# Experts 0 and 1 get their token columns by products with one-hot matrices; projection tiles and the second expert stream are requested in and right behind the scan

## The reference, cut to what matters

```
grp_prob = softmax(hf @ w_grp + b_grp);  grp = argmax(...)       # 4 groups
exp_logits = (hf @ w_exp + b_exp) of the chosen group            # 8 experts in it
top_logit, top_idx = lax.top_k(exp_logits, 2)
weights = p_grp * softmax(top_logit)
out[slot] = (silu(x[slot] @ w_gate[e]) * (x[slot] @ w_up[e])) @ w_down[e]
y = sum over the two chosen experts of weight * out
```

## Time and profile before

| | |
|---|---|
| median of 3 executions | 3174.89 us (3172.99 to 3177.99) |
| the profiled execution, its own time | 3174.74 us |
| its span, first to last instruction | 3173.0 us |
| TensorE busy | 2725.0 us (86%), weight loads 1970.6 us |
| VectorE, ScalarE, GpSimd busy | 1072.1, 527.9, 324.9 us |
| DMA | 638.61 MB, mean 201 GB/s |
| mean granted TensorE clock | 0.943 |

### The profile page before, as it was taken

How to read it: one execution, slowest core, us unless ns; L and a number is a source line. 1 busy time by engine, 2 the same in 40 slices (tenths; PEclk the granted TensorE clock), 3 DMA queues, 4 the chain that set the end, 5 groups by cost and what they waited for, 6 DMA issues and landing times. The chain is left out here.

```text
span 3173.0 us, 59030 instructions
## 1 busy us (share of the span) xinstructions
PE 2725.0 (86%) x25835; PEld 1970.6 (62%) x25835; DVE 1072.1 (34%) x2214; ACT 527.9 (17%) x1149; POOL 324.9 (10%) x358
## 2 busy tenths in 40 slices
PE   8999999989999997878786599798899976977775
PEld 7886766678868775444443244588888964544443
DVE  4563336435733213100001321565565422100002
ACT  1001132300011002000000100344444411000001
POOL 1000000000000001111110200232222201111110
PEclk9999998999999997989999799799999987999998
DMA  8684432057864237999998220000000049999994
GB/s 281 228 255 137 130 113 94 27 184 249 264 202 147 80 110 296 391 405 402 401 403 329 77 78 24 13 4 3 3 4 3 4 139 360 404 407 408 406 404 179
DMA packets 297238, 638.61 MB, mean 201 GB/s; under 512 B 29252, under 2 KB 198423, under 8 KB 262436
## 3 DMA queue, kind: packets, MB, share of 16 engines
q1 hardware_dynamic: 254896, 558.44, 48.2%
q10 hardware_dynamic: 30500, 61.96, 5.4%
q0 software_dynamic: 11600, 14.59, 1.5%
HBM read 634.79 MB, written 21.08 MB: 207 GB/s over the span
## 5 line engine op out<-in xcount | busy, mean ns | idle before, releaser
L2502 PE MATMUL bank<-expert_weights,ex_xt 128*64 128x256 f32 x2560 | 310.0, 390 | 74.3 <-DMA expert_weights<-in_moe_w_up_dram 52.6
L546 PE MATMUL bank<-u,weights 128*128 128x272 f32 (+1 forms) x1408 | 318.4, 390 | 11.3 <-DVEq L569 11.3
L2502 PEld LDWEIGHTS bank<-expert_weights,ex_xt 128*64 128x64 f32 x2560 | 203.3, 141 | 183.6 <-issue 113.9
L546 PEld LDWEIGHTS bank<-u,weights 128*128 128x128 f32 x1408 | 270.6, 192 | 58.9 <-DVEq L569 11.9
L1353 DVE SCALAR_TENSOR_TENSOR ada_acc<-ada_w,cond,ada_acc 128x512 f32 (+1 forms) x336 | 227.6, 746 | 1.6 <-PEq L518 1.6
L2420 DVE TENSOR_TENSOR ex_hidden<-ex_silu,bank 128x256 f32<-128x256 f32 x64 | 27.0, 421 | 569.7 <-ACT ex_silu L2551 569.7
L623 PE MATMUL bank<-rw_mixed,weights 128*128 128x512 f32 (+2 forms) x448 | 189.3, 584 | 31.9 <-DVEq L636 28.2
L2502 PE MATMUL bank<-weights,ex_xt 128*64 128x256 f32 x1280 | 165.9, 400 | 33.4 <-DMA weights<-in_moe_w_up_dram 24.4
L2523 PE MATMUL bank<-expert_weights,ex_hidden_turned 128*64 128x512 f32 x640 | 154.7, 626 | 20.7 <-DVE ex_hidden_turned L2423 20.7
L623 PEld LDWEIGHTS bank<-rw_mixed,weights 128*128 128x128 f32 (+1 forms) x448 | 84.2, 189 | 137.4 <-issue 135.5
L2551 ACT ACTIVATE ex_silu<-bank 128x256 f32<-128x256 f32 x64 | 24.6, 384 | 869.0 <-PE bank L2502 853.5
(11 more groups left out here) (602 smaller groups left out, 4292.2 us busy)
## 6 DMA issues: line engine op xcount, KB each, us to landing
expert_weights<-in_moe_w_gate_dram SPq DMA_DIRECT2D x80, 1024.0 KB, 24.4
expert_weights<-in_moe_w_up_dram SPq DMA_DIRECT2D x80, 1024.0 KB, 24.5
expert_weights<-in_moe_w_down_dram SPq DMA_DIRECT2D x80, 1024.0 KB, 24.6
ada_w<-in_ada_w_dram ACTq DMA_DIRECT2D x24, 2048.0 KB, 9.2
weights<-in_moe_w_down_dram SPq DMA_DIRECT2D x44, 1024.0 KB, 24.1
weights<-in_moe_w_gate_dram SPq DMA_DIRECT2D x40, 1024.0 KB, 23.9
weights<-in_moe_w_up_dram SPq DMA_DIRECT2D x40, 1024.0 KB, 24.0
weights<-in_ga_w_in_dram SPq DMA_DIRECT2D x32, 1024.0 KB, 5.7
```

The source lines that it names most:

```text
L546: last = nc.tensor.matmul(k.bank[b + side * NB][:, 0:N], w[:, f, c * P:(c + 1) * P], rhs[:, f, 0:N], start=(f == 5), stop=(f == 4))
L2502: last = nc.tensor.matmul(half_cols(k.bank[2 + side], t), xt[:, s, f * SLOTS:(f + 1) * SLOTS], w[:, q * 512 + t * 256:q * 512 + t * 256 + ...
```

## The change

In both mixtures:

- Experts 0 and 1 no longer get their rows by an inversion, a gather from DRAM and transposes. The token rows stay on chip (`hrow`: all but the last two blocks of 128 tokens in `h`, the last two in `xg`, which now has 128 partitions). For e = 0, 1 VectorE makes `chosen_by[:, e]`, a one-hot of the place times "assigned to e", and TensorE multiplies each row block (128x128 weights, per f and t) with it (64 moving columns), summed over the row blocks in banks 1 and 2. ScalarE copies the two results to `xt`, which now lives in `Route`. With T = 512 there are four row blocks, with T = 256 two.
- ScalarE copies and stores all row blocks without waiting for a buffer, and computes the exponentials afterwards. All stores count one semaphore, `ring.stored`.
- The inversion moves into expert 0 of the expert stage, behind its gate and up products; `tokens` and `pairs_of` are made there, then gathers 2 and 3 run, ahead of the scatters of slot lists. TensorE waits for them ahead of expert 1's down products. Tile 19 is requested at the head of the expert stage in layer 0, and in layer 1 at the head of the route stage.
- The slot lists are filled from a 64-wide memset tile by a DMA of shorter rows; the memset of `xg` goes.

In layer 1 only: the scan's scratch is named by the slots of `wo`, and a SyncE program in the scan's own block requests the four `wo` tiles once `rt_made` and `powered` have counted all heads; the empty block behind goes. The memory of the scan is released first, so `Route` and `place` come ahead of the projection, and the projection's SyncE program starts with the router's weights and 14 expert tiles.

```diff
@@ class ExpertRing, begin
-                for j in range(RING - tiles) if t == 0 else ():
-                    self.start(sp, a, l, 0, j)
                 self.start(sp, a, l, 0, RING - tiles + t)
@@ route_stage
-        hrow = k.h[:, :, :].rearrange("p c t -> p (c t)")[:, 0:2 * D].rearrange("p (s d) -> p s d", s=2)
+        h = k.h[:, :, :].rearrange("p c t -> p (c t)")
+        hrow = [h[:, t * D:(t + 1) * D] for t in range(TT - 2)] + [route.xg[:, t, :] for t in range(2)]
@@ route_stage, sync
-            route.load(sp)
-            for e in range(1, 3):
+            if l == 0:
+                route.load(sp)
+            for e in range(1, 3) if l == 0 else ():
...
-            for b in range(2):
-                sp.wait_ge(rstored[b], 16 * (TT // 2))
-            ring.start(sp, a, l, 3, 0)
+            if l == 1:
+                ring.start(sp, a, l, 3, 0)
@@ route_stage, tensor
-            pe.wait_ge(listed, 2)
-            for half in range(2):
-                for t in range(TT):
-                    for c in range(2):
-                        last = nc.tensor.matmul(k.bank[7][half * SLOTS:(half + 1) * SLOTS, 0:2 * NE], here[:, t, c, :],
...
+            pe.wait_ge(rcopied, 2 * TT)
+            for e in range(2):
+                pe.wait_ge(picked, e + 1)
+                for f in range(DC):
+                    for t in range(TT):
+                        last = nc.tensor.matmul(k.bank[1 + e][:, f * SLOTS:(f + 1) * SLOTS],
+                                                hrow[t][:, f * P:(f + 1) * P], chosen_by[:, e, t, :],
+                                                start=(t == 0), stop=(t == TT - 1))
+                last.then_inc(gathered, 1)
@@ route_stage, scalar
-                    if t >= 2:
-                        act.wait_ge(rstored[t % 2], 16 * (t // 2))
...
+            exponentials(act)
...
-            for b in range(2):
-                act.wait_ge(rstored[b], 16 * (TT // 2))
+            for e in range(2):
+                act.wait_ge(gathered, e + 1)
+                nc.scalar.activation(route.xt[:, e, :], k.bank[1 + e][:, :], ACT.Copy)
@@ route_stage, vector
             dve.wait_ge(placed, 1)
+            for e in range(2):
+                link(nc.vector.tensor_tensor(chosen_by[:, e, :, :], route.for_tokens(place[:, :], SLOTS),
+                                             pos[:, :, e:e + 1].broadcast_to([P, TT, SLOTS]), ALU.is_equal))
+                nc.vector.tensor_tensor(chosen_by[:, e, :, :], chosen_by[:, e, :, :],
+                                        A[:, :, e:e + 1].broadcast_to([P, TT, SLOTS]), ALU.mult).then_inc(picked, 1)
@@ experts_stage, sync
+            if l == 0:
+                sp.wait_ge(ring.stored, ring.rows)
+                ring.start(sp, k.a, l, 3, 0)
@@ experts_stage, vector
+                if e == 0:
+                    dve.wait_ge(inverted, 1)
+                    nc.vector.tensor_scalar(route.tokens[:, :], ...)
+                    nc.vector.tensor_scalar(route.pairs_of[:, :], ...).then_inc(named, 1)
@@ experts_stage, gpsimd
+            pool.wait_ge(named, 1)
+            pool.wait_ge(ring.stored, ring.rows)
+            for e in range(2, 4):
+                gather(k, route, pool, e)
             pool.wait_ge(destined, route.placed)
@@ experts_stage, tensor
-            turn(0)
             for e in range(NE):
...
-                if e + 1 < NE:
+                if e == 0:
+                    invert()
+                elif e + 1 < NE:
                     turn(e + 1)
...
+                if e == 1:
+                    pe.wait_ge(named, 1)
@@ rwkv
         scan_heads(k, q, r, kx, v, lw, la, gate)
-        with nc.Block() as block:
-            block.sync(k.stream.resume)
+        ctx.close()
+        route, ring = Route(k, 1, SEQ, held), k.ring
+        behind = ring.begin(k, a, 1, seg["wo"], 4)
+        ring.place(k, more)
+
+        def early(sp):
+            route.load(sp)
+            for n in [*range(RING - 4), *range(RING, ring.SLOTS - 1)]:
+                ring.start(sp, a, 1, *divmod(n, ring.PIECES))
@@ scan_heads
+            @block.sync
+            def _(sp):
+                sp.wait_ge(scan.rt_made, 2 * DC)
+                sp.wait_ge(scan.powered, 2 * DC)
+                k.stream.resume(sp)
```

More of the change, by code:

```diff
@@ L2177, in _ @@
                     .then_inc(consts, 1)
-            pool.memset(route.xg[:, :, :], 0.0).then_inc(consts, 1)
-            pool.wait_ge(consts, 17)
+            pool.wait_ge(consts, 16)
             pool.wait_ge(zeroed, 16)
-            pool.wait_ge(named, 1)
-            for b in range(2):
-                pool.wait_ge(rstored[b], 16 * (TT // 2))
-            for e in range(2):
-                gather(k, route, pool, e)
         @block.tensor
@@ L2254, in _ @@
             for t in range(TT):
-                if t == TT - 2 and TT > 2:
-                    exponentials(act)
                 for half in range(2):
@@ L2265, in _ @@
                 act.wait_ge(rcopied, 2 * t + 2)
[L2266 to L2268 removed]
+                act.dma_start(route.rows[t * P:(t + 1) * P, :], hrow[t]).then_inc(ring.stored, 16)
+            exponentials(act)
             act.wait_ge(diffed, 1)
             nc.scalar.activation(route.stat(5), route.stat(4), ACT.Exp).then_inc(exped, 1)
[L2271 to L2272 removed]
+            for e in range(2):
+                act.wait_ge(gathered, e + 1)
+                nc.scalar.activation(route.xt[:, e, :], k.bank[1 + e][:, :], ACT.Copy)
         @block.vector
@@ L2488, in turn, with invert @@
                 last.then_inc(turned, 1)
-            turn(0)
+            def invert():
+                for half in range(2):
+                    for t in range(TT):
+                        for c in range(2):
+                            last = nc.tensor.matmul(
+                                k.bank[7][half * SLOTS:(half + 1) * SLOTS, 0:2 * NE], route.here[:, t, c, :],
+                                route.whom[:, t, c, :], start=(t == 0 and c == 0), stop=(t == TT - 1 and c == 1))
+                last.then_inc(inverted, 1)
             for e in range(NE):
                 s = e % 2
-                pe.wait_ge(copied, e + 1)
+                if e >= 2:
+                    pe.wait_ge(copied, e - 1)
                 for j in range(2):
@@ L2699, in vector, with moe @@
         dve.wait_ge(self.put, count * 16 + 16)
-def moe(k, l, T):
+def moe(k, l, T, route, held, more):
     nc = k.nc
@@ L2705, in moe @@
     parts = [(t0, t1, k.gain2[:, v, :], k.mod[:, v, 3 * DC:4 * DC]) for v, (t0, t1) in enumerate(V)]
-    held, more = ExitStack(), ExitStack()
-    route = Route(k, l, T, held)
     with nc.sbuf_tensor(f"moe_h_{l}", [P, DC, T], F32) as hm:
-        k.ring.place(k, more)
+        if l == 0:
+            k.ring.place(k, more)
         route_stage(k, route, hm, parts)
@@ L2893, in rwkv @@
         linear_stage(k, "wo", seg["wo"], whole_tiles(DC, 256), lambda f: gate[:, f, :], SEQ, write, 4,
-                     behind=k.ring.begin(k, a, 1, seg["wo"], 4))
+                     behind=behind, early=early)
+    return route
 LEVELS = 6
```

121 lines of the change are left out of this document (63 added, 58 removed).

## The result

The changed kernel is slower: 3183.77 us (median of 13 executions, 3175.81 to 3189.37) against 3172.99 us (13 executions, 3165.43 to 3177.99), ratio 1.0031 with a 95% interval of 1.0021 to 1.0041. The forecast was 3175.4 us and "within 0.2%". The measured time is 8.4 us over it: inside the wide range of 3164 to 3188, but above the forecast's own 3171 to 3180 and above the 3181.3 that "within 0.2%" allowed. The profiled execution's span is 3181.2 us, before 3173.0, at the same mean clock of 0.943.

The account below looks back on a forecast made before the run. Expert stages were taken as bound by the DMA tile stream, which flows from each layer's first refill. Refills +13.1 and -12.4 us sum to +0.7 on 3174.74, so 3175.4 us; own range 3171 to 3180, wide range 3164 to 3188.

Parts of the forecast that it names:

- two refills carry the change: Expert 0, each layer: the first tile request into a freed ring slot moves everything behind; 13.1 us later, 12.4 us earlier.
- layer 0: Route stage to expert 0: one-hot products take 27.7 us from 1215.8, expert 0 at 1245.1, refill at 1251.0, 13.1 us later.
- The choice of the lower clock: One-hot products: TensorE stays at clock 0.50 (1.2 GHz), 0.216 us an instruction, 27.7 us in layer 0 instead of 14.1.
- Rival B: One-hot products: weight load doesn't hide the moving side, 0.32 us an instruction; layer 0 +13.2, layer 1 +6.6, 3195 us; 7%.
- layer 1: Projection starts 5.9 us earlier, one-hot products take 13.8 us; refill at 2647.9, 12.4 us earlier than 2660.27.
- Rival C: Layer 1: projection doesn't start earlier (late requests or a blocked SyncE); layer 1 gains 6.4 us only, 3181.4 us; 5%.
- Requested in the scan ... they are there; the DMA does next to nothing then.: Layer 1's scan: the four projection tiles arrive before the projection, which starts 5.9 us earlier; no cost to the scan counted.
- Sum: Whole kernel: layer 0's +13.1 and layer 1's -12.4 us give +0.7 us, so 3175.4 us.
- D: Starved stream in the expert stage: gather 2 lands over 9 us late, each further us costs one us; 3%.

Follow-up runs that it names:

- last-block kernel: Changed kernel with the one-hot products taken over the last block of 128 token rows alone; 3147.96 us, ratio 0.9917 to the kernel before.
- the products with 128 columns: Changed kernel with as many products, each over both experts' columns (128 for 64), one half of the result unused; 3160.54 us, ratio 0.9959 to before.
- requests after the scan: Changed kernel with the four projection tiles requested after the scan again, in a block of their own; 3187.09 us, ratio 1.0048 to the kernel before.
- four late: Changed kernel with the four projection tiles requested together but some 65 us later in the scan; 3174.76 us, ratio 1.0001 to the kernel before.
- the spaced kernel: Changed kernel with the four projection tiles requested one at a time inside the scan; 3174.52 us, ratio 1.0004 to the kernel before.

## Why the prediction was right and wrong

- **Right: two refills carry the change.** Expert stages run at DMA share 1.02 as before, and from expert 0 on the parts differ by 0.4 and 0.8 us. The last-block kernel shows the coupling.
- **Right: layer 0.** Products from 1216.10 (1215.8 said) for 27.6 us (27.7), expert 0 at 1245.42 (1245.1), refill at 1251.39 (1251.0). The choice of the lower clock, on L2209's row, was right. The Trainium skill ("TensorE: Matmul & The Clock Gate", Part 1: The HAM clock gate) says that sustained matmul activity releases the half rate; the products with 128 columns agree (1.00 behind 3.0 us in layer 0, 5.4 in layer 1), those with 64 don't in 27 us.
- **Rival B fell:** 0.213 us with 64 columns and with 128.
- **Right: layer 1,** refill 12.8 us nearer to the scan's end (12.4 said): 6.2 from the projection (requests in the scan put into the kernel before), the rest from the products.
- **Rival C, rightly small for this kernel,** is real: with the requests after the scan, SyncE blocked in a full queue held the stage's end for over 5 us. In the changed kernel it was 0.1 us short of doing so; the 5% was not far from coming true.
- **Wrong: "Requested in the scan ... they are there; the DMA does next to nothing then."** That cost term was zero and measures 3.3 to 5.4 us in the five runs with four tiles at once. I got it by laying each run's VectorE instructions, counted back from the scan's end, on those of before: the shift arises within ten of them. It is the pauses in TensorE and, in four of six kernels, the lower clock behind the first. In the changed kernel 5.2 of its 7.6 us are this.
- **The other 2.4 us** arise 21 to 33 us ahead of the scan's end, and they go with the granted clock. Windows at the same distance from the end, before and after:

```profile
2540.00:2550.00 10.00, 8.45 (x176) 7.40 (x173) 3.13 (x12) 2.29 (x9) 0.00 (x0) 0.83 0.01 3
```

```profile
2561.00:2571.00 10.00, 9.76 (x160) 9.08 (x158) 2.12 (x8) 1.84 (x7) 0.00 (x0) 0.50 0.01 3
```

  The clock is at 0.50 for some 3 us of this stretch before and for 10 after. In the kernels where it is so for 7 us the stretch is 1.0 to 1.1 us longer than before, in those with 10 us 1.7 to 2.4. Requests after the scan and four late have the 10 us too, without a stop at the requests, so these 2.4 us are not shown to come from the requests; what sets how long the clock stays down there is open. In all kernels but before and after, another stretch nearer to the end gives 0.9 to 1.0 us back.
- **Sum:** -12.8 in layer 1 and +12.9 in layer 0 cancel as forecast; the stall, with the 2.4 us, is what is left. The wide range held the result only because it left room for other causes: B, C and D, the slower rivals, are not what happened. Removing it gives 1.0004, no change, as the forecast said. That the medians fell by more (3183.8 to 3174.5) than 5.2 us is within the two intervals; part may lie in the 2.4 us, of which the spaced kernel has 1.1.

One execution is a poor witness of a total: five profiled executions with the same code up to layer 0's products started these between 1209.6 and 1219.6. The differences arise in the first 700 us. From first product to expert 0 all five took 29.3 us. Before and after happened to stand within 0.4 us of each other ahead of it.

## What to carry to other kernels

"The DMA is idle there" is no proof that a transfer is free: an engine that runs through straight-line code at full pace has its code fetched through the same DMA engines, so let requests of megabytes go one at a time there, or wait for a stretch where that engine idles. When a product is bound by the load of its weights, join the consumers of the same weights into one product: here it halved the instructions and also let the clock rise. And compare stage by stage from a common mark, since totals of single executions wander by more than the effect.

## What the hardware showed that I hadn't expected

- TensorE's granted clock stayed at 0.50 through 27 us of gap-free f32 products with 64 moving columns, and rose to 1.00 behind 3.0 us of the same products with 128 in layer 0, behind 5.4 us in layer 1.
- With two tiles (2 MB) requested together the next 16 KB code load came 7.8 us behind the last, where it comes 5.2 us behind without them, and TensorE stopped for 1.9 us; four tiles stopped it for 1.5 to 2.3 us and then again for 0.8 to 2.8 us, 255 or 256 instructions later.
- A pause of about 2 us in TensorE cost nearly as much again through the clock in four of six kernels: 0.50 for some 3 us behind it. In two it didn't fall there.
